# Fourteen modulation steps between attention items instead of between feed-forward rounds

## The chip, the cores and the metric

The kernel runs on one core of one Trainium2 chip. The metric is the device time of one execution in microseconds (us), of which several runs are shown; the profile is of one further execution. The engines are TensorE (PE, with its weight loads shown apart as PEld), VectorE (DVE), ScalarE (ACT), GpSimd (POOL) and SyncE (SP), which here issues the loads.

## The reference

Two transformer stacks run one after the other on 256 tokens of width 1024. The first is a hybrid block, a dense feed-forward, a state-space block and a mixture of experts. The second has two layers over 256 latent and 256 context tokens: layer 0 with an "even" mixer (a convolution beside differential attention), layer 1 with an "odd" one, each followed by a squared-ReLU feed-forward. Each layer is modulated by shifts, scales and gates that are a product of the condition with a matrix of 1024 x 6144. What bears on the change:

```python
for i in range(DEPTH):
    mods = jnp.split(cond_lat @ ada_w[i] + ada_b[i], N_MOD, axis=-1)
    ...
    h_lat = modulate_2(rms_norm(x, norm1_g[i]), sh1, sc1)
    ...                                        # even_mixer or odd_mixer
    x = x + gt1 * y_lat
    x = x + gt2 * squared_relu_mlp(modulate_2(rms_norm(x, norm2_g[i]), sh2, sc2), mlp_w1[i], mlp_w2[i])

def diff_attend(q, k, v, lam):
    s = jnp.einsum('bhmqd,bhmkd->bhmqk', q, k).astype(F32) * (DIFF_DQK ** -0.5)
    p = jax.nn.softmax(s, axis=-1)
    p = p[:, :, 0] - lam * p[:, :, 1]
    return jnp.einsum('bhqk,bhkv->bhqv', p.astype(v.dtype), v)

def squared_relu_mlp(h, w1, w2):
    return jnp.square(jax.nn.relu(h @ w1)) @ w2
```

## The kernel before

**Loads.** All weights lie in memory as slots of 1 MB (128 partitions x 2048 numbers), in one order that `schedule()` (L340) writes out by name. SP issues them in that order into a ring of five slots (L3571); a load waits until the engines that read the slot's former content have signalled that they are done. A slot asked for is so at most five ahead of the one in use.

**Modulation steps.** The products of the conditions with the modulation matrices are cut into steps and laid between other work. `Background` (L233) holds the list `MODS`; `bg.go(n)` makes the next n steps, and it is called at the same places in the lists of TensorE (`mod_pe`, L566), of VectorE (`mod_dve`, L617) and in `schedule()`. The matrix of layer 1, "ada1", has 24 slots and 25 steps. A step j on TensorE is first the sums of the previous step (L526: four matmuls of 128x2 out of `mrow`, behind a wait for VectorE's copy of the previous step), then the thin products of its own slot (L539: `thin` issues eight products of 128x256 on 32 columns of the array, which the trace shows as 16 matmuls) into columns 256 to 511 of a PSUM bank that the modulation keeps from its first step to its last. On VectorE it is one copy of 128x256 from that bank to `mrow` (L625). The last step has only the sums, and VectorE then makes the shifts and scales. ada1 must be done before the odd mixer's norm, which begins in round 9 of the second half of the feed-forward.

**The even mixer.** After its input products (ten slots `ev_in`) come 16 attention items t, four tiles of 128 queries times four heads; items 0 to 7 have 512 keys, items 8 to 15 have 256. The loop runs over t = 0 to 18 on each of three engines (`even_pe` from L2395, `even_act`, `even_dve` from L2553), and the work of an item is spread over several t. TensorE in t: `scores(t)` (L526, two products on 64 rows), `turned(t-2)` (transposes of the probabilities, L2349), `values(t-3)` (L526); and in t = 1 and 4 the sums for the convolution's mean and variance. VectorE in t: the two maxima of item t (L2558), then the combination of the two softmaxes of item t-1 (L2565 to L2568); and besides them the mean and centring (L2572, L2573, t = 2), reciprocals (L2577, t = 7 and 8) and normalisation (L2581, t = 9 and 10). ScalarE in t: exponentials (L2442), copies of transposed tiles (L2450), and of outputs (L2454, L2457). Behind the items stand one-column sums, the out products (L797, four slots `ev_out`) and the residual.

**The feed-forward of layer 0** (`mlp_pe` L2619, `mlp_dve`): two halves c of 256 tokens, each of 17 rounds r. Round r makes the up products of slot r (L526, 48 matmuls; in round 0 L772) and the down products of slot r-1 (L886, 48 matmuls). VectorE and ScalarE split each slot into two parts ahead of use (L868, L852), apply the squared ReLU (L2675, L2710, L2679, L2715), and VectorE adds the residual at the end of each half (L820). Each round ends with `bg.go(early_step(q, c, r))`, which before makes a step in all 17 rounds of the first half and in rounds 0 to 5 of the second.

**PSUM** has eight banks, taken in turn by `counts.take`; banks that are kept (the modulation's, the current attention output's, four of the down products) are passed over, and a taker waits until the former content was read.

Of the kernel before, what the change touches and what calls it, by code (L numbers as in the profile page):

```python
# [323 lines left out]
def ssm_steps(n):  # L324

    return 0 if n == 0 or 6 < n <= 12 and n % 2 == 0 else 1


def early_step(block, c, r):

    return 1 if block == 0 and (c == 0 or r < 6) else 0


def hybrid_steps(u):

    return 0 if u < 2 else 2 if 4 <= u < 8 else 1


def schedule():

    order = []

    def load(name, n=1):
        order.extend([name] * n)

    def step(name, slots, j):
        if j < slots:
            load(name)

    bg = Background(step)  # L350
    bg.finish("hyb_mod")
    for u in range(9):
        load("hyb_in")
        bg.go(hybrid_steps(u))
    load("cmp_w1", 4)
    bg.go(2)
    for u in range(3):
        load("hyb_in")
        bg.go(2)
    for i in range(4):  # L360
        load("hyb_out")
        bg.go(2 if i < 2 else 0)
    bg.finish("dense_mod")
    names = []
    for n in range(12):
        names += ["dense_g", "dense_u"] * (n < 11) + ["dense_d"] * (n > 0)
    made, used = 0, 0

    def ahead(n):
        nonlocal made, used  # L370
        while made < min(used + 1 + n, len(names)):
            load(names[made])
            made += 1
        used += 1

    for n in range(12):
        if n < 11:
            ahead(3)
            ahead(2)
            bg.go()  # L380
        if n:
            ahead(3)
        bg.go(n > 0)
    bg.finish("ssm_mod")
    for n in range(21):
        load("ssm_in")
        bg.go(ssm_steps(n))
    for i in range(8):
        load("ssm_out")
        bg.go(i < 6)  # L390
    bg.finish("moe_mod")
    bg.finish("ada0")
    order.extend(name for name, _ in RANKED.slots()[0])
    bg.finish("ada0")
    load("ev_in", 8)
    for n in range(2):
        bg.go()
        load("ev_in")
    load("ev_out", 4)
    for block in range(2):  # L400
        if block:
            bg.finish("ada1")
            load("od_in", 12)
            load("w3")
            load("dft")
            load("od_in", 3)
            load("dft")
            load("od_out", 4)
        names, made, used = [], 0, 0
        for c in range(2 - block):  # L410
            for n in range(17):
                names += [f"m{block}_1"] * (n < 16) + [f"m{block}_2"] * (n > 0)
        for c in range(2 - block):
            for n in range(17):
                if n < 16:
                    ahead(2)
                if n:
                    ahead(2)
                bg.go(early_step(block, c, n))
    return order  # L420
# [20 lines left out]
def program(nc, W, CS, SM, XIN, OUT):  # L441
    with ExitStack() as ctx:
# [76 lines left out]
        def mm(g, out, pairs, first=True, final=True, loose=False):  # L519

            n = len(pairs)
            for i, (l, r) in enumerate(pairs):
                kw = {"start": first and i == 0, "stop": final and i == n - 1}
                if loose:
                    kw["skip_group_check"] = True
                ins = g.matmul(out, l, r, **kw)  # L526
            return ins
# [1783 lines left out]
        def even_pe(g, s, bg):  # L2311
# [22 lines left out]
            def scores(t):  # L2334
                x, h = ev.idx[t]
                k0 = 0 if x < 2 else 256
                s.wait_ge("ev.rope", 4 + h, 2)
                for m in range(2):
                    b = counts.take("ev.s", t, m)
                    s.wait_emptied(b)  # L2340
                    q = slice(64 * m, 64 * m + 64)
                    mm(g, b.ap[:, 0:512 - k0], [(ev.qT[q, h, x * 128:x * 128 + 128], ev.kT[q, h, k0:512])]).then_inc(*s.done("ev.s_ps", t, m))

            def turned(i):
                x, h = ev.idx[i]
                b = counts.take("ev.pt", i)
                s.wait_emptied(b).wait_ge("ev.p", i)
                for k in range(4 if x < 2 else 2):
                    ins = g.transpose(b.ap[:, k * 128:k * 128 + 128], ev.sc[i % 3][0][:, k * 128:k * 128 + 128], ident)  # L2349
                ins.then_inc(*s.done("ev.pt_ps", i))  # L2350

            def values(i):
                x, h = ev.idx[i]
                k0 = 0 if x < 2 else 2
                if h == 0:
                    held[0] = counts.take("ev.o", x, keep=True)
                    s.wait_emptied(held[0])
                s.wait_ge("ev.pt", i).wait_ge("ev.vt", 1, 1)
                mm(g, held[0].ap[:, h * 128:h * 128 + 128], [(ev.vt[:, k0 + k, h * 128:h * 128 + 128], ev.PT[i % 2][:, k * 128:k * 128 + 128])
                                                             for k in range(4 - k0)]).then_inc(*s.done("ev.o_ps", i))  # L2360
                if h == 3:
                    counts.drop("ev.o", x)
# [32 lines left out]
            for t in ev_steps:  # L2395
                if t < 16:
                    scores(t)
                if 2 <= t < 18:
                    turned(t - 2)
                if 3 <= t < 19:  # L2400
                    values(t - 3)
                if t == 1:
                    b = counts.take("ev.mean")
                    s.wait_emptied(b).wait_ge("ev.tap", 3, 30)
                    mm(g, b.ap[:, :], [(ones, ev.C[:, m, :]) for m in range(4)]).then_inc(*s.done("ev.mean_ps"))
                if t == 4:
                    b = counts.take("ev.var")
                    s.wait_emptied(b).wait_ge("ev.sq")
                    mm(g, b.ap[:, :], [(ones, ev.sq[:, m * 512:m * 512 + 512]) for m in range(4)]).then_inc(*s.done("ev.var_ps"))
# [99 lines left out]
        def even_dve(g, s, bg):  # L2509
# [43 lines left out]
            for t in range(17):  # L2553
                if t < 16:
                    n = 512 if ev.idx[t][0] < 2 else 256
                    for m in range(2):
                        s.wait_ge("ev.s_ps", t, m)
                        g.tensor_reduce(ev.mx[:, 2 * t + m:2 * t + m + 1], counts.bank("ev.s", t, m)[:, 0:n], AX.X, MAX, negate=True).then_inc(  # L2558
                            *s.done("ev.mx", t, m))
                if t >= 1:  # L2560
                    i = t - 1
                    n = 512 if ev.idx[i][0] < 2 else 256
                    c = 2 * i
                    s.wait_ge("ev.ex", i, 1)
                    g.reciprocal(ev.su[:, c:c + 2], ev.su[:, c:c + 2]).then_inc(*s.done("ev.cmb", i, 0))  # L2565
                    s.own().tensor_tensor(ev.su[:, c + 1:c + 2], ev.su[:, c + 1:c + 2], lam[:, 3:4], MUL).then_inc(*s.done("ev.cmb", i, 1))
                    s.own().tensor_scalar(ev.sc[i % 3][0][:, 0:n], ev.sc[i % 3][0][:, 0:n], ev.su[:, c:c + 1], None, MUL).then_inc(*s.done("ev.cmb", i, 2))
                    s.own().scalar_tensor_tensor(out=ev.sc[i % 3][0][:, 0:n], in0=ev.sc[i % 3][1][:, 0:n], scalar=ev.su[:, c + 1:c + 2],  # L2568
                                                 in1=ev.sc[i % 3][0][:, 0:n], op0=MUL, op1=ADD).then_inc(*s.done("ev.p", i))
                if t == 2:  # L2570
                    s.wait_ge("ev.mean_ps")
                    g.tensor_scalar(ev.R, counts.bank("ev.mean")[:, :], 1.0 / 512, None, MUL).then_inc(*s.done("ev.mean", empties=("ev.mean",)))  # L2572
                    s.own().tensor_tensor(ev.C, ev.C, bc(ev.R.unsqueeze(1), (128, 4, 512)), SUB).then_inc(*s.done("ev.cent"))  # L2573
                if t in (7, 8):
                    c = slice((t - 7) * 256, (t - 7) * 256 + 256)
                    s.wait_ge("ev.root", t - 7)
                    g.reciprocal(RN[:, c], RN[:, c]).then_inc(*s.done("ev.rstd", t - 7))  # L2577
                if t in (9, 10):
                    m = slice(2 * (t - 9), 2 * (t - 9) + 2)
                    s.wait_ge("ev.rstd", 1)  # L2580
                    g.tensor_tensor(ev.C[:, m, :], ev.C[:, m, :], bc(RN[:, :].unsqueeze(1), (128, 2, 512)), MUL).then_inc(  # L2581
                        *(s.done("ev.ln") if t == 10 else s.done("ev.ln0")))
# [1287 lines left out]
```

## Time and profile before

| | us |
|---|---|
| median of three runs | 2906.77 (2904.12 to 2908.88) |
| the profiled execution | 2906.48 |
| its span, first to last instruction | 2904.4 |
| TensorE busy in it | 2770.5 (95%) |
| VectorE busy | 1187.1 (41%) |
| ScalarE busy | 709.1 (24%) |
| GpSimd busy | 48.3 (2%) |

The mean granted clock of TensorE is 0.978. The engines work side by side, so busy shares say little by themselves; the chain of work that ended last tells which engine set the time in a stretch. Times of the trace are counted from the span's start. The even mixer's items lie between 1745 and 1805 us, the feed-forward of layer 0 between 1876 and 2287 us. Ends of matmuls are modelled, and short groups of them can overlap by about 0.1 us.

### The profile page before, as it was taken

What the parts mean: (1) busy time and instruction counts of PE and PEld (TensorE: products, weight loads), DVE (VectorE), ACT (ScalarE), POOL (GpSimd) and SP (SyncE); (2) the same over time, 40 slices, a digit from 0 to 9 for tenths busy, and PEclk for the clock granted to TensorE, in tenths of its full rate; (3) what the DMA queues carried; (4) which work ended last, traced back from release to release, by engine and by line L of the source; (5) the groups of instructions that cost most, each with busy time, mean ns of one, the idle gap of its engine ahead of it and who ended that gap; (6) DMA issues with size and microseconds to landing.
All of it is one profiled execution on the core that took longest, in us unless ns stands there. A gap on an engine that the chain in (4) does not pass through costs nothing.

```text
span 2904.4 us, 49935 instructions
## 1 busy us (share of the span) xinstructions
PE 2770.5 (95%) x22276; PEld 1973.9 (68%) x22276; DVE 1187.1 (41%) x2055; ACT 709.1 (24%) x1136; POOL 48.3 (2%) x39
## 2 busy tenths in 40 slices
PE   8899999999999999999998997999999999998998
PEld 6789997877433333333333765899999965687998
DVE  4667764241301101101111686355455533553554
ACT  2234333140200000000001115243334312211443
POOL 0000000000000000000000000000000000131000
PEclk9899999999999999999999999999999998999999
DMA  8756765544999999999999120256654430010552
GB/s 335 301 195 255 275 253 210 195 155 173 362 380 420 421 420 420 421 420 421 420 413 380 58 102 15 104 214 262 253 225 162 144 116 16 16 62 19 186 180 82
DMA packets 95198, 686.88 MB, mean 236 GB/s; under 512 B 10624, under 2 KB 11776, under 8 KB 11904
## 3 DMA queue, kind: packets, MB, share of 16 engines
q1 hardware_dynamic: 94400, 681.37, 59.4%
q8 instruction: 177, 2.90, 0.4%
q10 hardware_dynamic: 576, 2.25, 0.2%
q14 instruction: 45, 0.37, 0.0%
HBM read 682.52 MB, written 1.05 MB: 235 GB/s over the span
## 4 chain that ended last, share of the span: by engine, by line
PE 85%; DMA 7%; DVE 5%; ACT 2%; issue 1%; SPq 0%; POOL 0%; ACTq 0%; DVEq 0%
PE ps L526 42%; PE ps L2049 14%; PE ps L886 12%; PE ps L797 6%; PE ps L2074 5%; DMA AR<-W 3%; DMA ring<-W 2%; PE ps L539 2%; PE ps L2077 2%; PE ps L772 1%; PE ps L2057 1%; DVE macc L642 0%; SPq L3571 0%; DMA XT<-XIN 0%; DMA sml<-SM 0%
## 5 line engine op out<-in xcount | busy, mean ns | idle before, releaser
L2049 PE MATMUL ps<-AR 128*32 128x512 f32 x2904 | 441.1, 595 | 11.4 <-DMA AR<-W 9.7
L526 PE MATMUL ps<-HT,ring 128*128 128x256 f32 (+1 forms) x1696 | 441.9, 421 | 2.7 <-ACT HT L715 2.7
L526 PEld LDWEIGHTS ps<-HT,ring 128*128 128x128 f32 x1696 | 322.9, 192 | 114.8 <-issue 75.1
L526 PE MATMUL ps<-FR,FR 128*128 128x256 f32 x3120 | 388.6, 284 | 0.0
L526 PEld LDWEIGHTS ps<-FR,FR 128*128 128x128 f32 x3120 | 378.5, 192 | 7.9 <-issue 7.8
L868 DVE TENSOR_TENSOR FR<-ring,FR 128x2048 fp32r<-128x2048 f32 x129 | 294.4, 2290 | 145.8 <-ACT FR L852 145.7
L886 PE MATMUL ps<-FR,FR 128*128 128x256 f32 x2832 | 349.3, 283 | 0.0
L886 PEld LDWEIGHTS ps<-FR,FR 128*128 128x128 f32 x2832 | 343.9, 192 | 0.4 <-issue 0.4
L2169 DVE TENSOR_TENSOR AR<-AR,ps 128x256 f32<-128x256 f32 x70 | 29.6, 423 | 678.8 <-ACT AR L2132 361.0
L2049 PE MATMUL ps<-ring,AR 128*32 128x512 f32 x1576 | 288.1, 593 | 5.8 <-DMA ring<-W 3.5
L2049 PEld LDWEIGHTS ps<-AR 128*32 128x32 f32 x2904 | 121.8, 110 | 228.1 <-issue 226.3
L852 ACT ACTIVATE FR<-ring 128x2048 fp32r<-128x2048 f32 x129 | 244.6, 1907 | 130.5 <-PE ps L886 86.7
L2132 ACT ACTIVATE AR<-ps 128x256 f32<-128x256 f32 x70 | 27.0, 386 | 659.1 <-PE ps L2049 659.1
L797 PE MATMUL ps<-AR,ring 128*128 128x256 f32 x768 | 172.9, 385 | 4.8 <-DVE AR L3513 2.2
L526 PE MATMUL ps<-AR 64*64 64x64 f32 (+9 forms) x2696 | 154.0, 249 | 17.1 <-DVE AR L3455 3.1
L797 PEld LDWEIGHTS ps<-AR,ring 128*128 128x128 f32 x768 | 146.7, 193 | 27.6 <-issue 7.1
L2049 PEld LDWEIGHTS ps<-ring,AR 128*32 128x32 f32 x1576 | 76.8, 110 | 121.5 <-issue 119.9
L526 PEld LDWEIGHTS ps<-AR 64*64 64x64 f32 (+3 forms) x2696 | 134.6, 153 | 32.3 <-issue 7.6
L2074 PE MATMUL ps<-AR 128*32 128x512 f32 x1088 | 128.0, 594 | 6.0 <-DMA AR<-W 3.5
L625 DVE COPY mrow<-ps 128x256 f32<-128x256 f32 x56 | 23.7, 423 | 199.8 <-PE ps L539 199.7
L642 DVE SCALAR_TENSOR_TENSOR macc<-ring,SC,macc 128x256 f32<-128x256 f32 x240 | 98.3, 478 | 0.0
L2074 PEld LDWEIGHTS ps<-AR 128*32 128x32 f32 x1088 | 33.5, 110 | 80.2 <-issue 70.2
(430 smaller groups left out, 2517.8 us busy)
## 6 DMA issues: line engine op xcount, KB each, us to landing
ring<-W SPq DMA_DIRECT2D x431, 1024.0 KB, 6.4
AR<-W SPq DMA_DIRECT2D x215, 1024.0 KB, 21.5
XT<-XIN ACTq DMA_DIRECT2D x2, 1024.0 KB, 8.5
cst<-CS SPq DMA_DIRECT2D x1, 1859.0 KB, 15.8
out<-XT SPq DMA_DIRECT2D x4, 256.0 KB, 2.2
sml<-SM SPq DMA_DIRECT2D x1, 970.5 KB, 11.9
cst<-CS ACTq DMA_DIRECT2D x1, 129.5 KB, 7.7
sml<-SM ACTq DMA_DIRECT2D x1, 16.0 KB, 5.3
```

The lines of the kernel that those rows point to most:

```text
L526: ins = g.matmul(out, l, r, **kw)
L539: ins = g.matmul(out[q, :], w[:, k, 0:32], rhs(k), start=k < 4, stop=k >= 4, skip_group_check=True)
L642: g.scalar_tensor_tensor(out=w, in0=by8(i)[:, m, :], scalar=SC[:, m:m + 1], in1=w, op0=MUL, op1=ADD).then_inc(*s.done(*name_, frees=(i,) i ...
L772: ins = g.matmul(out, l, r, start=k == 0 and j == 0 and begins, stop=k == 7 and j == 2, skip_group_check=True)
L797: ins = g.matmul(acc[m // 2].ap[:, h * 256:h * 256 + 256], w[:, kk, m * 128:m * 128 + 128], rhs(k), start=k == 0 and h == 0, stop=k == 2 * ...
L852: g.activation(self.pair(i)[0], src, ACT.Copy).then_inc(*s.done(self.x + ".hi", i))
L868: g.tensor_tensor(lo, src, hi.bitcast(F32), SUB).then_inc(*s.done(self.x + ".lo", i, frees=sl))
L886: ins = g.matmul(acc[m // 2].ap[:, h * 256:h * 256 + 256], l, r, start=i == 0 and kk == 0 and h == 0 and j == 0, stop=i == n - 1 and kk == ...
L2049: ins = g.matmul(bank.ap[group(i), :], mo.hg[e % 2][:, 4 * h + k, group(t)], w[n][:, k, :], start=j == 0 and k == 0, stop=j == 1 and k == ...
L2074: ins = g.matmul(acc[e][0].ap[group(q), :], rows[q // 2][:, kk, :], w[:, kk, q % 2 * 512:q % 2 * 512 + 512], start=i == 0 and kk == 0, sto ...
L2077: ins = g.matmul(acc[e][1].ap[group(q), :], rows[2][:, q // 2, :], w[:, q // 2, q % 2 * 512:q % 2 * 512 + 512], start=i == 0, stop=i == 13 ...
L2169: g.tensor_tensor(mo.hu[b % 2], mo.sg[b % 2], counts.bank(p + ".gu", b)[:, 256:512], MUL).then_inc(*s.done(p + ".hu", b, empties=(p + ".gu ...
```

## The change

The steps of ada1 are divided anew. Two are made before the attention items, as before. Fourteen are made in items t = 2 to 15: on TensorE between `scores(t)` and `turned(t-2)`, on VectorE behind the combination of item t-1. The remaining nine are made in rounds 0 to 8 of the first half of the feed-forward. The fourteen loads move from between the feed-forward's slots to ahead of the four `ev_out` slots.

```diff
@@ -326,9 +326,12 @@
     return 0 if n == 0 or 6 < n <= 12 and n % 2 == 0 else 1
 
 
+ATTENTION_STEPS = 14
+
+
 def early_step(block, c, r):
 
-    return 1 if block == 0 and (c == 0 or r < 6) else 0
+    return 1 if block == 0 and c == 0 and r < 23 - ATTENTION_STEPS else 0
 
 
 def hybrid_steps(u):
@@ -396,6 +399,7 @@
     for n in range(2):
         bg.go()
         load("ev_in")
+    bg.go(ATTENTION_STEPS)
     load("ev_out", 4)
     for block in range(2):
         if block:
@@ -2395,6 +2399,7 @@
             for t in ev_steps:
                 if t < 16:
                     scores(t)
+                bg.go(2 <= t < 2 + ATTENTION_STEPS)
                 if 2 <= t < 18:
                     turned(t - 2)
                 if 3 <= t < 19:
@@ -2567,6 +2572,7 @@
                     s.own().tensor_scalar(ev.sc[i % 3][0][:, 0:n], ev.sc[i % 3][0][:, 0:n], ev.su[:, c:c + 1], None, MUL).then_inc(*s.done("ev.cmb", i, 2))
                     s.own().scalar_tensor_tensor(out=ev.sc[i % 3][0][:, 0:n], in0=ev.sc[i % 3][1][:, 0:n], scalar=ev.su[:, c + 1:c + 2],
                                                  in1=ev.sc[i % 3][0][:, 0:n], op0=MUL, op1=ADD).then_inc(*s.done("ev.p", i))
+                bg.go(2 <= t < 2 + ATTENTION_STEPS)
                 if t == 2:
                     s.wait_ge("ev.mean_ps")
                     g.tensor_scalar(ev.R, counts.bank("ev.mean")[:, :], 1.0 / 512, None, MUL).then_inc(*s.done("ev.mean", empties=("ev.mean",)))
```

## Rows read from the trace of the kernel before

**Rows 1.** The page's part 4, the chain that ended last, by engine
```profile
PE 85%; DMA 7%; DVE 5%; ACT 2%; issue 1%; SPq 0%; POOL 0%; ACTq 0%; DVEq 0%
```

**Rows 2.** The chain in order of time, feed-forward: start us, us, what
```profile
2055.15 1.00 PE ps L539 x16
...
2067.86 0.34 PE ps L526 x4
2068.20 1.00 PE ps L539 x16
...
2174.12 5.76 PE ps L526 x48
...
2185.64 5.76 PE ps L526 x48
```

**Rows 3.** Stretches: length, busy PE, PEld, DVE, ACT, POOL; clock, DMA, GB/s
```profile
1752.00:1802.00 50.00, 35.66 (x196) 22.48 (x194) 39.95 (x94) 30.95 (x83) 0.00 (x0) 0.93 0.00 1
1876.00:2085.00 209.00, 209.00 (x1847) 199.00 (x1846) 108.30 (x99) 83.77 (x80) 0.00 (x0) 1.00 0.64 246
```

**Rows 4.** The chain in order of time, attention items, VectorE's maxima and centring
```profile
1752.07 1.27 DVE AR L2558 x2
...
1755.55 2.29 DVE AR L2573
...
1781.91 0.60 DVE AR L2558 x2
...
1791.63 0.66 DVE AR L2558 x2
...
1793.47 0.66 DVE AR L2558 x2
...
1795.31 0.66 DVE AR L2558 x2
...
1798.98 0.67 DVE AR L2558 x2
```

**Rows 5.** Timeline of TensorE, items: start, us, what [idle before, releaser]
```profile
1768.41 0.66 PE L2349 MATMUL ps<-cst,AR 128*128 128x128 f32 x4
1768.90 2.12 PE L526 MATMUL ps<-AR 128*128 128x128 f32 x12
...
1795.37 0.44 PE L2349 MATMUL ps<-cst,AR 128*128 128x128 f32 x2 [0.32 <-DVE AR L2568]
1795.64 1.24 PE L526 MATMUL ps<-AR 128*128 128x128 f32 x8
```

**Rows 6.** Timeline, first products of the feed-forward's second half
```profile
2090.88 6.02 PE L772 MATMUL ps<-FR,FR 128*128 128x256 f32 x48 [1.33 <-DVE XT L820]
```

**Rows 7.** Timeline, the last modulation step ahead of the items
```profile
1726.23 0.63 PEld L526 LDWEIGHTS ps<-cst,mrow 128*128 128x128 f32 x4
...
1726.88 0.59 PEld L539 LDWEIGHTS ps<-ring,SC 128*32 128x32 f32 x16
...
1727.88 3.32 PEld L526 LDWEIGHTS ps<-AR,cst 128*128 128x128 f32 x16 [0.41 <-issue]
...
1728.02 0.42 DVE L625 COPY mrow<-ps 128x256 f32<-128x256 f32 x1 [7.52 <-PE ps L539]
```

**Rows 8.** DMA issues from 1700 to 1900: KB each, median us to landing
```profile
ring<-W SPq DMA_DIRECT2D x17, 1024.0 KB, 6.2
```

**Rows 9.** Behind the items: one stretch, then TensorE's timeline
```profile
1805.00:1808.00 3.00, 3.00 (x16) 3.00 (x16) 0.00 (x0) 2.98 (x5) 0.00 (x0) 0.51 0.00 0
...
1805.77 3.41 PE L526 MATMUL ps<-cst,AR 128*128 128x1 f32 x16
1809.04 8.55 PE L797 MATMUL ps<-AR,ring 128*128 128x256 f32 x32
1817.43 1.84 PE L526 MATMUL ps<-cst,AR 128*128 128x1 f32 x16
1819.13 7.15 PE L797 MATMUL ps<-AR,ring 128*128 128x256 f32 x32
```

## The prediction

> **What bounds the kernel now.** I read the chain of waits first: TensorE carries 85% of it and VectorE 5% [rows 1]. So what matters is where TensorE is the chain and where it isn't, and I read the same chain in order of time for both stretches that the change touches.
>
> In the feed-forward (1876 to 2285 us) the chain is nothing but TensorE. A round with a modulation step begins at 2055.15 and the next at 2068.20, which is 13.05 us. Once the steps have run out, the up half of a round begins at 2174.12 and the next at 2185.64, which is 11.52 us [rows 2]. The stretch table shows 209.0 of 209 us busy on TensorE, while VectorE is busy 108.3, ScalarE 83.8 and the DMA engines at 0.64 [rows 3]. Every microsecond of TensorE work taken out here shortens the kernel.
>
> In the attention items the chain changes hands. In the stretch 1752 to 1802, TensorE is busy 35.66 of 50 us and VectorE 39.95, at a mean granted clock of 0.93, and no weights are moving [rows 3]. The last eight items follow each other at VectorE's pace: one item's maxima start at 1793.47, the next one's at 1795.31, 1.84 us apart [rows 4]. TensorE's own work for such an item runs from 1795.37 to 1796.88, 1.51 us [rows 5]. An early item (512 keys) takes it from 1768.41 to 1771.02, 2.61 us [rows 5].
>
> **What is moved.** There are 25 steps of ada1 (24 slots and a last one with sums only). Two stand before the items, both before and after; of the 23 in the feed-forward, 14 go to items 2 to 15 and 9 stay (r = 0 to 8 of the first half). All engines' lists and the loads agree (2 + 14 + 9). Nothing is added or dropped in total. Each moved step is, on TensorE, 4 matmuls of the sums on the previous `mrow` and 16 thin ones; on VectorE, one copy of 128x256 out of PSUM; and on SP's queue, one load of 1 MB.
>
> **Feed-forward, gain 21.4 us.** A round shrinks by 13.05 - 11.52 = 1.53 us, and 14 x 1.53 = 21.4. The last, sums-only step now falls in round 8, so all 14 moved ones are whole. Next in line in a round would be VectorE at about half of it [rows 3], so nothing is late behind TensorE. I give this term 21.0 to 21.8.
>
> **Turn of the halves, gain 1.3 us.** After the last down products of the first half, VectorE stands at the copy of a step that TensorE issues only behind those products, and the residual of the first half stands behind that copy. TensorE's next up products then wait 1.33 us for the residual to empty their bank [rows 6]. With the step gone, the residual can begin during the down products. Following the bank turns, the modulation bank also comes free after round 8, and up(16) then takes a bank last held by up(12), not one of the residual's. The wait has nothing left to come from: gain 1.3, between 0 and 1.6.
>
> **The price of a step in the items.** The step just before the items shows it among plain matmuls: from the first weights of its sums at 1726.23 to the first weights of what follows at 1727.88, 1.65 us of TensorE, and 0.42 us of VectorE for the copy [rows 7]. Fourteen steps ask for 23.1 us of TensorE and 14 x 0.46 = 6.4 us of VectorE, a hand-over included.
>
> **Attention, loss 7.5 us.** A floor first. TensorE has 50 - 35.66 = 14.3 us free, and the clock of 0.93 gives back at most 0.07 x 50 = 3.5 us if it stays up. So even a perfect filling leaves 23.1 - 14.3 - 3.5 = 5.3 us, and 8.8 without the clock. By items:
> - Items 2 to 7 (maxima from 1752.07 to 1781.91, 29.8 us [rows 4]): TensorE needs 6 x (2.61 + 1.65) = 25.6, which leaves 4.2 for the variance's eight matmuls. That just fits. One wait will not fill: the sums of item 4 need the copy of item 3, which stands on VectorE behind the centring of 2.29 us [rows 4] and one more combination. I take +0.5.
> - Items 8 to 10 (1781.91 to 1791.63) are VectorE's, with the reciprocals and the normalisation; the copies add 3 x 0.46, and the first sums wait for them: +1.8.
> - Items 11 to 15 turn from VectorE's pace to TensorE's: 1.51 + 1.65 = 3.16 in place of 1.84 us, four distances from maxima to maxima (1791.63 to 1798.98 [rows 4]): 4 x 1.32 = 5.3, less 0.7 in the first, where VectorE is still the later one: +4.6.
> - Behind the last item, one more copy ahead of the last combination: +0.5.
>
> Sum 7.4, taken as 7.5; bounds 5.3 and 13. The upper one adds 14 x 0.4 for one hand-over per item that isn't hidden.
>
> **The new wait.** Each item's sums on TensorE wait for VectorE's copy of the step before. Queued behind them are the thin products, the transposes and the value products, for which ScalarE and then VectorE's later items wait. VectorE is through with the copy about 1.84 + 0.46 = 2.3 us after a late item's scores, and TensorE comes to the next sums 3.16 us after them, so in the late items the copy is there first. The copy in turn waits for the thin products, but VectorE has 1.2 us or more of its own work before it.
>
> **Loads.** No weights move during the items now [rows 3], and a 1 MB load lands 6.2 us after its issue [rows 8]. The ring has five slots. Slots 2 to 6 of ada1 come in before item 2, each later one is asked for five items ahead (14 us or more), and the fourteen ask for 1 MB per 3 to 4 us. The four slots of `ev_out` are asked for as items 11 to 14 free theirs and the first is wanted only behind item 18; the first feed-forward slot follows item 15, some 70 us ahead of its use. Cost 0; without that cover, each late load would cost up to its 6.2 us.
>
> The Trainium skill ("TensorEngine Tiling (Array Packing)", Key Properties) says that changing the tiling mode drains TensorE. That speaks against this change, as the scores run on 64 rows and the thin products on 32 columns. The 1.65 us in plain surroundings against 1.53 in the feed-forward [rows 7, 2] already hold two such changes; if each cost another 0.1 in the items, 28 of them would make the loss 10.3 in place of 7.5.
>
> **The sum.** The profiled execution took 2906.48 us (span 2904.4 and 2.1 around it), the median of the runs is 2906.77: no difference. 2906.5 - 21.4 - 1.3 + 7.5 = 2891.3; I say **2891**.
>
> **Rivals.**
> - **The clock stays up behind the items (20%).** Now the clock falls after TensorE's idle time at the end of the items: 0.51 in 1805 to 1808, where 16 one-column matmuls take 3.41 us against 1.84 the next time, and the out products 8.55 against 7.15 [rows 9]. Items 11 to 15 will leave TensorE hardly idle. If the 1.2 GHz stretch is gone, 1.57 + 1.40 = 3.0 us more are won: 2888. Against it: the gap of two microseconds behind ScalarE's last transposed tile stays, and no step stands in items 16 to 18. That the clock is the low one by default and activity raises it is also what the Trainium skill says ("TensorE: Matmul & The Clock Gate", What's actually happening).
> - **The hand-overs show (14%).** Sums wait for copies and copies for thin products in most items, at the upper bound: +13 in place of +7.5, 2897. For it: VectorE is busy 80% already [rows 3], and the early items have waits both ways.
> - **Nothing is hidden (3%).** The items grow by the whole 23.1: 2907. Against it: 14.3 us of idle TensorE.
> - **Slower (3%).** The copy's place in VectorE's list turns each item into a serial round: TensorE's step, then the copy before the next step may begin, and nothing of the idle time is used. The items grow by 14 x (1.65 + 0.42) = 29 us, and the kernel ends at 2913. It decides from a growth of 22.7 / 14 = 1.62 us per item. Against it: scores of the next item are issued ahead of the sums, so VectorE always has an item's work while TensorE has a step.
>
> **How the numbers follow.** The forecast has 60%, with 2888.5 to 2894.5 for it alone. The range of 8 in 10 runs from 2885 (clock kept, floor of the items) to 2897.5 (hand-overs). A measurement of this kernel tells about 0.2%, 5.8 us, from no change, so faster means below 2901: all of the forecast, the clock and nearly all of the hand-overs, 0.91; within it 0.05; slower 0.04.
>
> **What would show it.** In the profile after: rounds of 13.05 us up to round 7 of the feed-forward and of 11.52 from round 9 on; no wait of L772's products for the residual at the turn; copies of `mrow` in every item from 2 to 15; late items some 3.1 us apart with TensorE without gaps; TensorE waiting for the copy only around items 3, 4 and 8 to 11; the distance from the first scores to the first feed-forward products longer by 7.5 us. The prediction is wrong if late items are over 3.6 us apart (hand-overs), if loads end waits in the items, or if rounds without steps are longer than 11.52.

## The result and the profile after

The changed kernel takes 2892.56 us (median of four runs, 2887.84 to 2895.38) against 2907.82 before; the ratio is 0.9949, with a 95% interval of 0.9937 to 0.9961. That is 15.3 us less, where the forecast's terms add up to 15.2 (21.4 + 1.3 - 7.5). The profiled execution took 2892.33 us with a span of 2890.3.

In the changed kernel the lines behind the call put into `schedule()` stand four later up to the items: L530 is L526 of before, L543 is L539, L629 is L625, L801 is L797, L890 is L886, and the transposes are L2353. VectorE's maxima of an item are L2563, five later.

The page's chain by engine is nearly as in [rows 1]:

```profile
PE 86%; DMA 6%; DVE 5%; ACT 2%; issue 1%; SPq 0%; POOL 0%; ACTq 0%; DVEq 0%
```

The chain in order of time (start us, us, what) shows the feed-forward with steps, without them, and the turn of the halves; it answers to [rows 2] and [rows 6]:

```profile
1959.59 0.34 PE ps L530 x4
1959.93 1.00 PE ps L543 x16
1960.93 5.95 PE ps L530 x48
...
1972.64 0.34 PE ps L530 x4
...
2010.71 5.76 PE ps L530 x48
2016.47 5.76 PE ps L890 x48
2022.23 5.76 PE ps L530 x48
...
2074.07 11.52 PE ps L890 x96
2085.59 5.76 PE ps L776 x48
```

A round with a step lasts 1972.64 - 1959.59 = 13.05 us, one without 2022.23 - 2010.71 = 11.52. At the turn the products of L776 begin the moment the last down products end (2074.07 + 11.52 = 2085.59): the 1.33 us are gone.

TensorE's timeline (start, us, what, and in brackets the idle time before and who ended it) answers to [rows 5] and [rows 9]. First the wait at item 4, then two late items, then what follows the items:

```profile
1761.33 2.12 PE L530 MATMUL ps<-AR 128*128 128x128 f32 x12
1765.33 0.61 PE L530 MATMUL ps<-cst,mrow 128*128 128x2 f32 x4 [1.88 <-DVE mrow L629]
...
1769.24 4.27 PE L530 MATMUL ps<-AR,cst 128*128 128x512 f32 x8
...
1803.53 0.61 PE L530 MATMUL ps<-cst,mrow 128*128 128x2 f32 x4
1804.07 1.07 PE L543 MATMUL ps<-ring,SC 128*32 128x256 f32 x16
1805.07 0.44 PE L2353 MATMUL ps<-cst,AR 128*128 128x128 f32 x2
1805.34 1.24 PE L530 MATMUL ps<-AR 128*128 128x128 f32 x8
1806.51 0.61 PE L530 MATMUL ps<-cst,mrow 128*128 128x2 f32 x4
...
1815.71 0.71 PE L530 MATMUL ps<-AR 128*128 128x128 f32 x4 [1.73 <-ACT AR L2455]
1816.26 1.84 PE L530 MATMUL ps<-cst,AR 128*128 128x1 f32 x16
1817.96 8.84 PE L801 MATMUL ps<-AR,ring 128*128 128x256 f32 x32
```

A late item is 1806.51 - 1803.53 = 2.98 us, without a gap on TensorE. VectorE, which set the pace before, now waits: its maxima of such an item carry an idle time in front.

```profile
1803.63 0.76 DVE L2563 TENSOR_REDUCE AR<-ps 128x1 f32<-128x256 f32 x2 [0.92 <-PE ps L530]
...
1806.61 0.76 DVE L2563 TENSOR_REDUCE AR<-ps 128x1 f32<-128x256 f32 x2 [0.72 <-PE ps L530]
```

**Where the time went.** I cut each profile at four places, so that parts which have nothing to do with the change can't blur the comparison: the first scores of item 0 on TensorE; the start of the last transposes; the start of the first feed-forward products; the end of the last down products.

| us | before | changed | |
|---|---|---|---|
| span's start to first scores | 1745.35 | 1749.34 | +3.99 |
| first scores to last transposes | 56.71 | 63.75 | +7.04 |
| last transposes to feed-forward | 73.86 | 72.04 | -1.82 |
| feed-forward | 411.08 | 388.21 | -22.87 |
| rest of the span | 617.40 | 616.96 | -0.44 |

The first line is not counted as an effect of the change: the list of work is the same there, and among the eleven profiles of this study it lies between 1743.24 and 1749.94. That it is chance is not shown, though. The changed kernel's two profiles agree within 0.5 us, its variant at the turn has 1749.01, and the three kernels with seventeen steps have 1743.24 to 1744.71. If it goes with the kernel, the change gains 17.65 - 3.99 = 13.7 us; the interval of the medians holds both numbers. The changed stretches together are 17.65 us shorter, and the difference of the two profiled executions is 3.6 less than that because of the other parts. For the same reason the experiments are compared by these stretches first and by their medians second.

### The profile page after: what moved, and what is told of

It reads as the page before. It is cut to its first block, busy times and chain, and to the rows that moved or that the text cites. A ratio compares the mean times of both kernels' runs of the same rounds, so it can differ in the third digit from the quotient of the medians.

```text
span 2890.3 us, 49935 instructions
## 1 busy us (share of the span) xinstructions
PE 2770.7 (96%) x22276; PEld 1973.5 (68%) x22276; DVE 1186.3 (41%) x2055; ACT 709.9 (25%) x1136; POOL 48.3 (2%) x39
## 4 chain that ended last, share of the span: by engine, by line
PE 86%; DMA 6%; DVE 5%; ACT 2%; issue 1%; SPq 0%; POOL 0%; ACTq 0%; DVEq 0%
PE ps L530 42%; PE ps L2053 15%; PE ps L890 12%; PE ps L801 6%; PE ps L2078 5%; DMA AR<-W 3%; DMA ring<-W 2%; PE ps L543 2%; PE ps L2081 2%; PE ps L776 1%; PE ps L2061 1%; DVE macc L646 0%; DMA XT<-XIN 0%; SPq L3577 0%; ACT AR L1761 0%
## 5 line engine op out<-in xcount | busy, mean ns | idle before, releaser
L530 PE MATMUL ps<-HT,ring 128*128 128x256 f32 (+1 forms) x1696 | 443.4, 422 | 1.7 <-ACT HT L719 1.7
L530 PEld LDWEIGHTS ps<-HT,ring 128*128 128x128 f32 x1696 | 324.2, 193 | 114.5 <-issue 75.0
L530 PE MATMUL ps<-FR,FR 128*128 128x256 f32 x3120 | 387.4, 284 | 0.0
L530 PEld LDWEIGHTS ps<-FR,FR 128*128 128x128 f32 x3120 | 378.7, 192 | 3.0 <-issue 2.9
L890 PE MATMUL ps<-FR,FR 128*128 128x256 f32 x2832 | 349.0, 283 | 0.0
L890 PEld LDWEIGHTS ps<-FR,FR 128*128 128x128 f32 x2832 | 343.8, 192 | 0.0
L801 PE MATMUL ps<-AR,ring 128*128 128x256 f32 x768 | 173.3, 386 | 4.9 <-DVE AR L3519 2.2
L530 PE MATMUL ps<-AR 64*64 64x64 f32 (+9 forms) x2696 | 153.0, 249 | 16.1 <-DVE AR L3461 3.2
L801 PEld LDWEIGHTS ps<-AR,ring 128*128 128x128 f32 x768 | 147.0, 193 | 27.7 <-issue 7.2
L530 PEld LDWEIGHTS ps<-AR 64*64 64x64 f32 (+3 forms) x2696 | 134.9, 153 | 30.4 <-issue 7.4
L629 DVE COPY mrow<-ps 128x256 f32<-128x256 f32 x56 | 23.5, 420 | 184.2 <-PE ps L543 184.1
```

The lines of the kernel that those rows point to most:

```text
L801: ins = g.matmul(acc[m // 2].ap[:, h * 256:h * 256 + 256], w[:, kk, m * 128:m * 128 + 128], rhs(k), start=k == 0 and h == 0, stop=k == 2 * ...
L890: ins = g.matmul(acc[m // 2].ap[:, h * 256:h * 256 + 256], l, r, start=i == 0 and kk == 0 and h == 0 and j == 0, stop=i == n - 1 and kk == ...
```

## The experiments

**Early steps alone.** Six steps in items 2 to 7; 17 in the feed-forward.

```diff
-ATTENTION_STEPS = 14
+ATTENTION_STEPS = 6
```

> Only six steps go to the items, those of t = 2 to 7 (512 keys); 17 stay in the first half of the feed-forward, round 16 among them. Theory A (a step costs what TensorE has not free in its item, so early steps are nearly free): from first scores to the last transposes +1.5 us against before (58.2 in place of 56.7), from there to the feed-forward as before, feed-forward 411.1 - 6 x 1.53 = 401.9 with the 1.33 us wait at the turn of the halves still there; together 7.7 us below before, 2900. Theory B (every step costs the same half microsecond, 7.0 / 14, by hand-overs): items +3.0, together 6.2 below before.

Measured: 2901.45 us against 2906.21, ratio 0.998 (0.9969 to 0.9991), 4.8 us less. The items took 56.75 us, as if there were no steps in them (56.71), and from first scores to the feed-forward 130.63 against 130.57. So the six early steps add nothing to the measured stretch, where theory B had +3.0. That is not idle time alone, however. Among these items the clock fell twice in the kernel before (granted 0.61 in 1760 to 1763, 0.54 in 1775 to 1778), and here it stayed up (1.00 from 1767 to 1779). TensorE's timeline before, and then here:

```profile
1760.67 1.11 PE L2349 MATMUL ps<-cst,AR 128*128 128x128 f32 x4 [2.88 <-DVE AR L2568]
...
1763.53 3.88 PE L526 MATMUL ps<-AR,cst 128*128 128x512 f32 x8
...
1773.87 3.49 PE L526 MATMUL ps<-AR 128*128 128x128 f32 x12
```

```profile
1767.47 0.66 PE L2353 MATMUL ps<-cst,AR 128*128 128x128 f32 x4
...
1768.86 3.60 PE L530 MATMUL ps<-AR,cst 128*128 128x512 f32 x8
...
1775.48 2.12 PE L530 MATMUL ps<-AR 128*128 128x128 f32 x12
```

From the transposes to the next scores TensorE took 1767.35 - 1760.67 = 6.68 us before and 1772.38 - 1767.47 = 4.91 here, and for the later products 3.49 and 2.12: 3.1 us, and before both pieces were on the chain. Two variants below without early steps also lost 3.1 us there. So an estimate at a like clock is that the six steps cost up to 3.1 us and the clock gave as much back. That would be the half microsecond a step of theory B; it is the late variant, below, that speaks against B. No run has these steps together with the clock of before, so the split is not shown.

The feed-forward was a miss: 404.08, not 401.9. The last step, which makes the shifts and scales, now stands at the turn:

```profile
2093.24 0.26 DVE L654 TENSOR_TENSOR M_ada<-ps,sml 128x96 f32<-128x96 f32 x1 [3.23 <-PE ps L530]
2093.53 0.78 DVE L658 SCALAR_TENSOR_TENSOR N_ada<-M_ada,sml 128x8 f32<-128x8 f32 x4
2094.22 3.22 DVE L824 SCALAR_TENSOR_TENSOR XT<-ps,M_ada,XT 128x256 f32<-128x256 f32 x8
...
2095.15 7.50 PE L776 MATMUL ps<-FR,FR 128*128 128x256 f32 x48 [1.95 <-DVE XT L824]
```

VectorE makes them ahead of the residual, TensorE waits 1.95 us in place of 1.33, and the products behind it take 7.50 in place of 6.02 [rows 6], with a granted clock of 0.61 in 2096 to 2099: 0.6 + 1.5 = 2.1 of the 2.2 us that were missing.

**Late steps alone.** Eight steps in items 8 to 15; 15 in the feed-forward. Both engines' calls change alike.

```diff
-ATTENTION_STEPS = 14
+ATTENTION_STEPS = 8
-                bg.go(2 <= t < 2 + ATTENTION_STEPS)
+                bg.go(8 <= t < 8 + ATTENTION_STEPS)
```

> Eight steps go to the items, those of t = 8 to 15; 15 stay in the feed-forward (rounds 0 to 14). Theory A (TensorE takes over from VectorE in the late items): items +5.3 us against before (62.0), late items 2.98 us apart; feed-forward 411.1 - 8 x 1.53 - 1.33 = 397.5; one-column sums behind the items at full clock (-1.6); together about 9.8 us below before, 2898. Theory B (half a microsecond per step): items +4.0, together 11.1 below.

Measured: 2899.02 us, ratio 0.9976 (0.9967 to 0.9986). Items 61.97 us (62.0 expected), feed-forward 397.41 (397.5), from first scores to the feed-forward 135.67, where the changed kernel with all fourteen took 135.79. So theory A holds for the items, and B, with 4.0, doesn't. The eight late steps cost 5.1 us, and the six early ones on top of them 0.1. That 0.1 is the sum of two effects of the clock and not a price of the steps: the items grow by another 1.78 us, and the part behind them shrinks by 1.66. The one-column sums took 2.86 us here, where 1.84 were expected, so the clock came back only in part, and the out products behind them took 9.47 (8.84 in the changed kernel). There is also no wait at the turn here, though the modulation's bank is still kept then until round 14 and the up products of the second half take a bank of the residual's, as before.

**The turn.** One of the nine remaining steps is put back into round 16, and the last one into round 0 of the second half.

```diff
-    return 1 if block == 0 and c == 0 and r < 23 - ATTENTION_STEPS else 0
+    return 1 if block == 0 and (c == 0 and (r < 7 or r == 16) or c == 1 and r == 0) else 0
```

> As the changed kernel, with fourteen steps in the items, but of the nine in the feed-forward one stands in round 16 of the first half and one in round 0 of the second (rounds 0 to 6, 16, and 0). Theory A (the wait at the turn comes from the step between the last down products and the residual): the wait of TensorE for the residual is back, 0.9 to 1.8 us, feed-forward 389.5 to 390 in place of 388.2, items unchanged. Theory B (the wait came from the turn of the banks or from something else): no wait there and 388.2 as in the changed kernel.

Measured: 2897.18 us, ratio 0.9963 (0.995 to 0.9976); feed-forward 393.69, which is 5.5 more than the changed kernel's and not 1.3. TensorE's timeline has two waits:

```profile
2085.96 6.02 PE L776 MATMUL ps<-FR,FR 128*128 128x256 f32 x48 [1.33 <-DVE XT L824]
2091.82 0.50 PE L530 MATMUL ps<-cst,mrow 128*128 128x2 f32 x4
2094.95 7.30 PE L530 MATMUL ps<-FR,FR 128*128 128x256 f32 x48 [2.63 <-DVE M_ada L654]
```

The first is the 1.33 us of before, to the hundredth. The second I had not foreseen: the next up products take the bank that the modulation has just given back, and wait until VectorE has made the shifts and scales out of it; behind that wait they run at 7.30 in place of 5.9 us. 1.33 + 2.63 + 1.4 = 5.4. With the late variant above, where the bank is the same as before but no step stands at the turn, this shows that the step is the cause of the 1.33 us. The variant with three steps behind the items, which again has a step in round 16, has the wait of 1.33 us, too. The turn of the banks, which the prediction also named, isn't needed for it; it may have a small share of its own, 0.31 us, in the next variant.

**Seventeen steps, up to item 18.** VectorE's last two copies stand behind its loop.

```diff
-ATTENTION_STEPS = 14
+ATTENTION_STEPS = 17
+            bg.go(2)
             for x in range(4):
                 if x % 2 == 0:
                     rstd_dve(g, s, f"ev.rms{x // 2}", 9 + 4 * x, 8)
```

> Seventeen steps in the items, t = 2 to 18 (VectorE's copies of the last two behind its loop); six stay in the feed-forward. Theory A (TensorE's idle 2.2 us behind the last items can be filled, and filling it keeps the clock at 2.4 GHz): feed-forward 388.2 - 3 x 1.53 = 383.6; from first scores to the feed-forward +1.5 against the changed kernel (135.8 to 137.3) with the first out products at 7.1 us in place of 8.8, so 3 us below the changed kernel. Theory B (the three steps stand in the way of the last transposes and the tail, and each costs its whole 1.6 us): +4.9 in front and -4.6 behind, no difference to the changed kernel.

Measured: 2881.74 us (2880.57 to 2886.8), ratio 0.9921 (0.9907 to 0.9935). From first scores to the feed-forward 134.52 us, 1.27 less than with fourteen steps although three more are in it. TensorE's timeline behind the items:

```profile
1811.50 0.71 PE L530 MATMUL ps<-AR 128*128 128x128 f32 x4
1812.05 1.84 PE L530 MATMUL ps<-cst,AR 128*128 128x1 f32 x16
1813.75 7.15 PE L801 MATMUL ps<-AR,ring 128*128 128x256 f32 x32
```

No idle time is left, and the first out products take 7.15 us, at full clock. Theory A holds in kind; I had expected 1.5 us more in front than there were with fourteen, and it was 1.3 less; 1.7 us of that difference are the early items, which ran at full clock this time (see the repeat below). The feed-forward took 384.96, not 383.6. The median is 10.8 us below the changed kernel's first one; the two stretches give 1.27 + 3.25 = 4.5 of it, and most of the rest lies ahead of the first scores (1744.71 against 1749.34).

**The changed kernel again**, without an edit, on another chip than the experiments so far.

> The changed kernel once more, without any edit. In its first profile the maxima of item 5 began 24.10 us behind those of item 0, where two variants with the same code up to there took 22.43. Theory A (a fall of TensorE's clock that hits one execution and not another): 22.4 us are as likely as 24.1 here, with the variance's eight matmuls at 3.6 us in place of 4.3; and the growth of the stretch from first scores to the feed-forward lies between 3 and 5.2 us over before. Theory B (it belongs to the kernel): 24.1 again.

Measured: 2892.04 us (2888.64 to 2892.9), ratio 0.995 (0.9937 to 0.9964), so the result stands. The stretches repeated to 0.02 us: 63.76, 135.80, 388.22. The maxima of item 5 began 24.10 us behind the first again, which theory A, an accident of single executions, does not explain; but theory B doesn't either, as the list of work up to there is the same in the variants with six and seventeen steps, where it was 22.4. What differs is the clock. Of the stretch tables (length, busy PE, PEld, DVE, ACT, POOL, granted clock, DMA, GB/s), the first is the changed kernel's, the second that with seventeen steps, at the same work:

```profile
1766.00:1769.00 3.00, 3.00 (x27) 2.42 (x24) 2.27 (x6) 1.96 (x5) 0.00 (x0) 0.70 0.29 60
1769.00:1772.00 3.00, 3.00 (x8) 1.48 (x7) 0.00 (x0) 0.00 (x0) 0.00 (x0) 0.74 0.71 295
```

```profile
1762.00:1765.00 3.00, 3.00 (x24) 2.05 (x17) 1.67 (x4) 1.32 (x4) 0.00 (x0) 1.00 0.47 137
1765.00:1768.00 3.00, 3.00 (x10) 0.98 (x8) 0.00 (x0) 0.00 (x0) 0.00 (x0) 1.00 0.54 218
```

Both have the same 1.88 us of idle time ahead of it. In four profiles (fourteen steps twice, the turn and the doubled steps) the clock fell to 1.2 GHz there for a time, in three (six steps, and seventeen steps with the rest in rounds 0 to 5 or 2 to 7) it stayed at 2.4. In the three kernels without early steps, the one before among them, it fell there after 2.88 us of idle time. Why it repeats with the kernel stays open.

**Seventeen steps, the rest in rounds 2 to 7.**

```diff
-    return 1 if block == 0 and c == 0 and r < 23 - ATTENTION_STEPS else 0
+    return 1 if block == 0 and c == 0 and 2 <= r < 8 else 0
```

> Seventeen steps in the items as in the variant with t = 2 to 18, and the six left in rounds 2 to 7 of the feed-forward in place of 0 to 5. Theory A (the 1.4 us that the feed-forward of that variant was too long come from round 6, where VectorE has the norm of the second half and TensorE ran into it for want of a step, and from the up products of the second half, whose bank was one of the residual's because the modulation's bank came free after round 5): 384.96 - 1.36 = 383.6 us. Theory B (both waits stay, wherever the steps stand): 385. From first scores to the feed-forward 134.5 as there.

Measured: 2884.61 us (2880.49 to 2885.36) against 2905.54, ratio 0.9926 (0.9913 to 0.994), and 7.4 below the changed kernel's 2892.04 on the same chip, of which the two stretches give 1.27 + 4.60 = 5.9. Feed-forward 383.62 as expected, the stretch in front 134.53. So the 1.4 us were where I had looked for them. In the variant with rounds 0 to 5 the chain left TensorE for VectorE's norm:

```profile
1942.73 1.76 DVE RN L747
...
1952.24 2.30 DVE FR L872
...
1954.68 5.98 PE ps L530 x48
```

TensorE's timeline has 0.64 us of idle time before these products, and at the turn a wait of 0.31 us for the residual. With the steps two rounds later both are gone. TensorE then comes to these products when VectorE is already through; and at the turn its bank is no longer one of the residual's, though no run changes the bank alone. The medians of the two variants can't be told apart (2881.74 and 2884.61, on different chips).

**Two steps in each late item.** One step each in t = 2 to 10, two in t = 11 to 15, the last four in rounds 4 to 7. Both engines' calls change alike.

```diff
-ATTENTION_STEPS = 14
+ATTENTION_STEPS = 19
-                bg.go(2 <= t < 2 + ATTENTION_STEPS)
+                bg.go((2 <= t < 16) + (11 <= t < 16))
-    return 1 if block == 0 and c == 0 and r < 23 - ATTENTION_STEPS else 0
+    return 1 if block == 0 and c == 0 and 4 <= r < 8 else 0
```

> Nineteen steps in the items: one in each of t = 2 to 10 and two, one straight behind the other, in each of t = 11 to 15; the four left stand in rounds 4 to 7 of the feed-forward. The feed-forward should be 388.2 - 5 x 1.53 = 380.6. Theory A (in the late items TensorE is the bound, and a second step costs just its own 1.5 us): late items 4.5 us apart, from first scores to the feed-forward 134 to 136 + 7.5 = 142 to 143.5, the kernel as fast as the changed one. Theory B (the second step's sums wait for the copy of the first, which stands on VectorE behind the maxima and the combination, 2.3 us behind the scores): late items 5.2 to 5.4 us apart, 4 us slower than the changed kernel.

Measured: 2899.49 us (2890.61 to 2904.64), 7.5 above the changed kernel on the same chip; feed-forward 380.55 as expected, from first scores to the feed-forward 153.19, 17.4 more. Theory B holds in kind, and both missed the size: the first late items were 6.98 us apart, the last two 5.40. TensorE's timeline of a slow one:

```profile
1803.99 0.61 PE L530 MATMUL ps<-cst,mrow 128*128 128x2 f32 x4
1804.53 1.07 PE L543 MATMUL ps<-ring,SC 128*32 128x256 f32 x16
1806.41 0.61 PE L530 MATMUL ps<-cst,mrow 128*128 128x2 f32 x4 [0.82 <-DVE mrow L629]
1806.95 1.79 PE L543 MATMUL ps<-ring,SC 128*32 128x256 f32 x16
1808.67 0.69 PE L2353 MATMUL ps<-cst,AR 128*128 128x128 f32 x2
1809.15 1.88 PE L530 MATMUL ps<-AR 128*128 128x128 f32 x8
1810.97 0.61 PE L530 MATMUL ps<-cst,mrow 128*128 128x2 f32 x4
```

The second step's sums wait for the first one's copy in every item, 1.57 us in the first and 0.81 or 0.82 in the other four. And the thin products take 1.79 in place of 1.07, the item's others 1.88 in place of 1.24: the granted clock is down for part of each of the first three items (0.69 in 1806 to 1809). Where it stayed up, the same item took 1823.35 - 1817.94 = 5.41 us:

```profile
1817.94 0.61 PE L530 MATMUL ps<-cst,mrow 128*128 128x2 f32 x4
...
1820.36 0.61 PE L530 MATMUL ps<-cst,mrow 128*128 128x2 f32 x4 [0.81 <-DVE mrow L629]
...
1823.35 0.61 PE L530 MATMUL ps<-cst,mrow 128*128 128x2 f32 x4
```

So 2.98 + 1.5 + 0.8 = 5.3 is the price with the hand-over, as theory B had it, and the clock adds 1.6 to an item where it falls.

**The copy of item 3 first.** Seventeen steps, rounds 2 to 7, and on VectorE alone:

```diff
             for t in range(17):
+                bg.go(t == 3)
...
-                bg.go(2 <= t < 2 + ATTENTION_STEPS)
+                bg.go(2 <= t < 2 + ATTENTION_STEPS and t != 3)
```

> As the variant with seventeen steps in items 2 to 18 and six in rounds 2 to 7, but VectorE makes the copy of item 3's step ahead of that item's maxima and combination, straight behind the centring. Theory A (TensorE's one long wait in the items, 1.88 us at the sums of item 4, is the copy's place in VectorE's list): the wait is below 0.4 us, the maxima of item 5 begin some 1.5 us earlier (20.9 in place of 22.4 us behind the first), and the stretch from first scores to the feed-forward is 133.0 in place of 134.5; feed-forward 383.6. Theory B (the wait only changes its name: the transposes of item 2 wait for the combination instead): 22.4 and 134.5 as there.

Measured: 2883.42 us (2881.08 to 2884.34), ratio 0.9922 (0.9908 to 0.9936). The maxima of item 5 began 21.17 us behind the first in place of 22.44, and the stretch took 133.25 in place of 134.53. TensorE's timeline at item 4:

```profile
1758.51 0.61 PE L530 MATMUL ps<-cst,mrow 128*128 128x2 f32 x4
...
1760.45 0.66 PE L2353 MATMUL ps<-cst,AR 128*128 128x128 f32 x4 [0.34 <-DVE AR L2574]
```

The 1.88 us were the copy's place in VectorE's list, and the stretch gains 1.28 of them; 0.34 of them come back at the transposes, as theory B had feared for all of them. Its median can't be told from the variant without it.

**Three steps behind the items alone.** t = 16 to 18; twenty in the feed-forward.

```diff
-                bg.go(2 <= t < 2 + ATTENTION_STEPS)
+                bg.go(16 <= t < 16 + ATTENTION_STEPS)
-    return 1 if block == 0 and c == 0 and r < 23 - ATTENTION_STEPS else 0
+    return 1 if block == 0 and 17 * c + r < 23 - ATTENTION_STEPS else 0
```

with ATTENTION_STEPS = 3 and VectorE's copies as with seventeen.

> Only three steps go to the items, those of t = 16 to 18, behind the last scores; twenty stay in the feed-forward (rounds 0 to 16 of the first half, 0 to 2 of the second). Theory A (TensorE's idle time there takes them in, and with it filled the clock doesn't fall behind the items): the one-column sums at 1.84 in place of 3.41 us and the first out products at 7.15 in place of 8.55, so from first scores to the feed-forward 130.6 - 3.0 + 0.5 = 128.1; feed-forward 411.1 - 4.6 = 406.5, the wait at the turn included; together 7 us below before. Theory B (the clock falls all the same, as TensorE has been idle a third of the time in the late items): 131, together 4 below before.

Measured: 2901.12 us against 2906.93, ratio 0.9978 (0.9969 to 0.9987), 5.8 less. The stretch from first scores to the feed-forward is 128.47 us, 2.1 shorter than before with three steps more in it, and the feed-forward 406.49. The out products in question:

```profile
1810.39 1.84 PE L530 MATMUL ps<-cst,AR 128*128 128x1 f32 x16
1812.09 7.15 PE L801 MATMUL ps<-AR,ring 128*128 128x256 f32 x32
```

That separates the clock from the late items: these were as idle as before, only the gap behind them was filled, and the clock stayed at 2.4 GHz. Theory B is wrong.

## Why the prediction was right

**Feed-forward, forecast -21.4 and -1.3.** Measured -22.87 together, against -22.7. The round's 1.53 us held in every variant, apart from the waits named there (rounds 0 to 5, and the last step at the turn). The wait at the turn was the step's, as forecast; the bank's turn, offered beside it, wasn't needed for the 1.33 us (the late variant has no wait at the old bank) and is worth at most the 0.31 us of the variant with rounds 0 to 5. The wait for the last step's bank, 2.63 us, shows that it could have worked the other way.

**Loads, forecast 0.** Held: no load ends a wait on TensorE in the items, even with two steps in each.

**Items, forecast +7.5.** Measured +7.04 up to the last transposes, but put together otherwise, read from the starts of the maxima. The closeness is in part luck, as a miss of +1.2 stands against three of -0.8, -0.6 and -0.2:
- Items 2 to 8: +1.7, forecast +0.5. The early variant, with the same steps here, grew by 0.04; what the changed kernel has beyond it is the fall of the clock in the variance's products and those ahead of them (6.57 us in place of 4.91). But before, the clock's falls had cost 3.1 us in these items. By the estimate above the steps cost up to 3.1 and the clock gave 1.4 back. The forecast knew that the clock could give back up to 3.5 us and had it in its floor; its sum by items set full-clock durations (2.61 an item) against a distance of 29.8 us with falls in it, and had no term for a fall. The wait of item 4 for the copy behind the centring came as told, 1.88 us. It was paid only in part out of time in which TensorE waited for VectorE before, too: without it the stretch is 1.28 us shorter.
- Items 8 to 11: +1.0, forecast +1.8. The copies cost VectorE 0.33 to 0.34 each on the chain, not 0.46, and no first wait came.
- Items 11 to 15: +4.0, forecast +4.6. This term was mis-sized by the price of a step: 2.98 us per item makes it 2.98 - 1.51 = 1.47 us, not the 1.65 of [rows 7]. That row began at the first weight load, which in the items runs beside the matmuls ahead of it. The Trainium skill's rule on the drain at a change of the tiling mode ("TensorEngine Tiling (Array Packing)", Key Properties) had made me weigh a further charge; at 1.47 here against 1.53 in the feed-forward, the trace shows no further charge.
- The last item: +0.3, forecast +0.5.

**Behind the items, forecast 0, and -3.0 in a rival.** Measured -1.82: -1.57 from the one-column sums at full clock, -0.34 from the last value products ahead of them, also at full clock, -0.20 from a shorter wait for ScalarE's last tile, +0.29 from the out products, in which the clock fell after all, only later than before. The rival had the mechanism, and about half its price came.

**The sum.** The changed stretches gave 17.65 us where 15.2 were forecast, 2.3 of it in front of the feed-forward (5.22 in place of 7.5). The kernel's median shows 15.3, next to the 15.2 of the forecast; that it comes so near is luck, as the terms miss by 2.5 us and the other parts of the kernel take about as much back. The interval of the medians, 11 to 18 us, holds all of these numbers, and the front part varies by more than their difference between profiles. The rival "hand-overs show" wasn't needed with one step per item and came true with two.

## What to carry to other kernels

Background work belongs where the bounding engine of the kernel is idle, and its price there is that of the item's two engines side by side: in the late items here an item costs what its busier engine needs, steps included. Six steps in items with slack left the time of the items as it was and took 9.2 us of rounds away, though about 3 us of that stretch were the clock's falls, which went away with the idle time; eight in items that turned from VectorE's pace to TensorE's cost 5.1 and saved 12.2, and a second step in the same items cost 5.41 - 2.98 = 2.4 us each at full clock and 17.4 / 5 = 3.5 us in fact. Short gaps ahead of dense matmuls are worth filling beyond their own length, as the clock then can stay up: three steps put into the gaps behind the last items shortened their stretch by 2.1. The last step of such a series, the one that hands its bank back, needs a place where no one wants the bank or the engine right behind it.

## What the hardware showed unexpectedly

- The clock fell to 1.2 GHz for a time in the middle of work, 1.88 us of idle time before it, in four profiles and not in three others with the same instructions up to there and the same gap; it cost 1.7 us each time. What decided between the two groups no run here shows. The Trainium skill ("TensorE: Matmul & The Clock Gate", What's actually happening) has the clock set by how busy TensorE has been recently. The list of work up to there is the same in both groups, so this alone does not tell them apart.
- With two steps per late item and an idle time of 0.82 us in most of them (1.57 in the first), the clock was down for part of the first three (0.55 to 0.88 in several stretches of 3 us), and the thin products of their second steps took 1.65 to 1.93 us in place of 1.07. In the last two, with the same idle time, it stayed up.
- The part ahead of the first scores, the same in all kernels, ended between 1743.24 and 1749.94 us in the profiles, and two profiles of the same kernel differed by 0.5 us only. Whether it goes with the kernel no run here shows.
